# Sums of squares of a head from two rounded parts, four pieces of work at other places, and gates of 516 instead of 528 columns

## What is computed

```python
# a head of block one, and of block two alike
o = o * lax.rsqrt(jnp.mean(o * o, axis=-1, keepdims=True) + EPS)
o = o.reshape(...) * norm_w
out_a = (o * jax.nn.silu(g))
...
# Mamba-2: gate by z, mean square over each of two groups of 512 channels
y = y.reshape(bsz, length, M2_WIDTH) * jax.nn.silu(z)
yg = y.reshape(bsz, length, M2_GROUPS, M2_WIDTH // M2_GROUPS)
yg = yg * lax.rsqrt(jnp.mean(yg * yg, axis=-1, keepdims=True) + EPS)
...
h = h + jnp.concatenate([out_a, out_b], axis=-1) @ w_out
...
return y[:, N_META:, :]
```

## Time and profile before

| what | value |
|---|---|
| three runs, us | 1803.2, 1803.99, 1805.36 |
| the profiled execution: its time, us | 1804.95 |
| the profiled execution: its span, first to last instruction, us | 1803.2 |
| mean granted TensorE clock, share of full | 0.995 |
| PE busy, us (share of the span) | 1770.3 (98%) |
| DVE, ACT, POOL busy, us | 1168.4, 709.7, 10.4 |

### The profile page before, as it was taken

How to read it: one execution, slowest core, us unless ns; L and a number is a source line. 1 busy time by engine, 2 the same in 40 slices (tenths; PEclk the granted TensorE clock), 3 DMA queues, 4 the chain that set the end, 5 groups by cost and what they waited for, 6 DMA issues and landing times.

```text
span 1803.2 us, 27256 instructions
## 1 busy us (share of the span) xinstructions
PE 1770.3 (98%) x11004; PEld 1534.0 (85%) x11004; DVE 1168.4 (65%) x1798; ACT 709.7 (39%) x1085; POOL 10.4 (1%) x10
## 2 busy tenths in 40 slices
PE   8999999999999999999999999999999999999997
PEld 5777777778878888888899989999988999999885
DVE  5666656656567777633576766688788877777333
ACT  5333433332343333333545454543454433333221
POOL 0000000000000000000000000000000000000000
PEclk9999999999999999999999999999999999999998
DMA  6222222223333333332222122222212223333331
GB/s 200 79 74 79 82 82 84 82 81 94 93 87 98 96 94 93 103 96 94 70 84 71 59 69 63 70 71 63 79 60 80 74 94 94 95 94 87 101 93 59
DMA packets 44540, 154.23 MB, mean 86 GB/s; under 512 B 6000, under 2 KB 6256, under 8 KB 44416
## 3 DMA queue, kind: packets, MB, share of 16 engines
q1 hardware_dynamic: 44416, 152.50, 27.8%
HBM read 150.39 MB, written 2.10 MB: 85 GB/s over the span
## 4 chain that ended last, share of the span: by engine, by line
PE 81%; DVE 9%; ACT 4%; issue 2%; DVEq 1%; ACTq 1%; DMA 0%; POOL 0%; POOLq 0%; SPq 0%
PE ps L607 80%; ACT arena L911 2%; DVE arena L1272 2%; PE ps L611 2%; DVE w_lo L1269 1%; DVE arena L1279 1%; DVEq L1774 1%; ACTq L1252 1%; ACT w_hi L911 1%; DVE r_bc L1269 1%; ACT L916 0%; DVE arena L1269 0%; DVE u_lo L1464 0%; ACT u_hi L911 0%; DVE h_res L1269 0%
## 5 line engine op out<-in xcount | busy, mean ns | idle before, releaser
L607 PE MATMUL ps<-u_hi,w_hi 128*128 128x264 f32 (+3 forms) x2376 | 649.3, 326 | 12.1 <-DVE u_lo L1464 8.8
L607 PE MATMUL ps<-u_hi,w_lo 128*128 128x264 f32 (+3 forms) x2376 | 641.5, 323 | 0.0
L607 PE MATMUL ps<-u_lo,w_hi 128*128 128x264 f32 (+3 forms) x2376 | 639.9, 323 | 0.0
L607 PEld LDWEIGHTS ps<-u_hi,w_hi 128*128 128x128 f32 (+1 forms) x2376 | 395.9, 189 | 58.2 <-issue 14.7
L1269 DVE TENSOR_TENSOR w_lo<-w_raw,w_hi 128x1024 fp32r<-128x1024 f32 x280 | 342.5, 1223 | 153.6 <-ACT w_hi L911 142.2
L607 PEld LDWEIGHTS ps<-u_hi,w_lo 128*128 128x128 f32 (+1 forms) x2376 | 395.3, 188 | 36.9 <-issue 1.8
L607 PEld LDWEIGHTS ps<-u_lo,w_hi 128*128 128x128 f32 (+1 forms) x2376 | 395.1, 188 | 36.4 <-issue 0.8
L911 ACT ACTIVATE w_hi<-w_raw 128x1024 fp32r<-128x1024 f32 x280 | 294.7, 1053 | 327.4 <-PE ps L607 319.0
L1279 DVE SCALAR_TENSOR_TENSOR ffn<-full,par,ffn 128x512 f32<-128x512 f32 (+2 forms) x176 | 132.3, 751 | 81.0 <-ACT ffn L911 77.8
L911 ACT ACTIVATE arena<-arena 128x528 f32<-128x528 f32 (+10 forms) x189 | 96.5, 533 | 216.0 <-DVE arena L1272 91.8
L911 ACT ACTIVATE ffn<-full,par 128x512 f32<-128x512 f32 x88 | 67.8, 770 | 277.9 <-DVE full L1272 277.9
(11 more groups left out here) (140 smaller groups left out, 1488.2 us busy)
## 6 DMA issues: line engine op xcount, KB each, us to landing
w_raw<-weights SPq DMA_DIRECT2D x280, 512.0 KB, 3.6
h_res<-xT SPq DMA_DIRECT2D x8, 256.0 KB, 4.9
outT<-h_res SPq DMA_DIRECT2D x8, 256.0 KB, 2.1
cst<-consts SPq DMA_DIRECT2D x1, 730.0 KB, 8.6
seg<-consts SPq DMA_DIRECT2D x1, 256.0 KB, 8.7
par<-params SPq DMA_DIRECT2D x1, 240.0 KB, 5.7
msk<-cmask SPq DMA_DIRECT2D x1, 128.0 KB, 9.0
h_res<-metaT SPq DMA_DIRECT2D x1, 64.0 KB, 8.5
```

The lines of the kernel that those rows point to most:

```text
L607: return nc.tensor.matmul(out, lhsT, rhs, start=start, stop=stop)
```

## The change

**The head's sum.** Behind the copies of `head_c` ACT waits for its own squares and writes their rounded part into the head's place in `y_hi` (block one) or `v_hi` (block two), which is free at that time. A new DVE step `square_low` writes the rest into `y_lo` or `v_lo`. PE multiplies a column of rounded ones, repeated 128 times, with both parts. In block one `square_low` stands behind `head_c`; in block two inside the next head's `prep`, for the last head behind group ("mz", 0).

**Narrower.** Groups hg and mz and all that is done with gates, heads' roots and Mamba outputs cover columns 12 to 527.

**Four moves.** (1) the memsets `second_start 4` from behind hf 0 to behind hq 0; (2) ACT's `slab_behind` of group ("oh", 2) behind step a of tile 1; (3) ACT's tanh of group ("mz", 4) and its `slab_behind` behind `ssm_sum 0`; (4) on DVE the reading of group ("om", (0, 4)), and on ACT and POOL the square of tile 6, behind step a of tile 7. Besides, the scratch tile `m_cbm` lies elsewhere in the arena.

```diff
-    ... ("mz", 6): "silu mx 7; c 6", ("om", (0, 4)): "a 7",
+    ... ("mz", 6): "silu mx 7; c 6", ("om", (0, 4)): "a 7; sq 6; out 4",
@@ columns
-    return (USED, T2) if kind in ("oh", "om", "up2") else (0, T2)
+    return (USED, T2) if kind in ("oh", "om", "up2", "hg", "mz") else (0, T2)
@@ schedule
             put(*where, ("head_" + stage, h))
+            if stage == "c":
+                put(*where, ("square_low", h))
...
-    put("hf", 0, ("second_start", 4))
+    put("hq", 0, ("second_start", 4))
...
-                pieces += [("ssm_sum", 0)] if n == 4 else []
+                pieces += [("ssm_sum", 0), ("z_tanh", 4), ("slab_behind", GROUP_OF[where])] if n == 4 else []
                 pieces.append(("ssm_gate", n))
                 pieces += [("ssm_v2", n)] if n == M2_T - 1 else []
-                pieces.append(("ssm_sq", n))
+                pieces += [("ssm_sq", n)] if n != 6 else []
+            if where == ("oh", 2) and stage == "a":
+                pieces.append(("slab_behind", GROUP_OF[where]))
...
+    after[GROUP_OF[("mz", 0)]].append(("square_low", last))
@@ tensor engine, head_d
-                pe.wait_ge(o_ok, n + 1)
-                last = mm(ps[:, 6, :], ones[:, :], g_osq if gla else h_osq[:, META:T2])
+                pe.wait_ge(sq_lo_ok, n + 1)
+                _, hi, lo = square_parts(n)
+                m = 0 if gla else META - USED
+                every = ones_r[:, :].broadcast_to((P, P))
+                mm(ps[:, 6, :], every, hi[:, m:], stop=False)
+                last = mm(ps[:, 6, :], every, lo[:, m:], start=False)
                 if not gla:
-                    last = mm(ps[:, 7, 416:432], ones[:, :], h_osq[:, 0:META])
+                    mm(ps[:, 7, 416:420], every, hi[:, 0:m], stop=False)
+                    last = mm(ps[:, 7, 416:420], every, lo[:, 0:m], start=False)
@@ scalar engine
-                if GROUPS[g][0] != "hf":
+                if GROUPS[g][0] != "hf" and GROUPS[g][:2] not in (("mz", 4), ("oh", 2)):
                     slab_behind(g)
...
                 last.then_inc(o_ok, 1)
+                act.wait_ge(o_ok, n + 1)
+                x, hi, _ = square_parts(n)
+                f(hi, x, ACT.Copy).then_inc(sq_hi_ok, 1)
@@ vector engine, prep
                 last.then_inc(ready, 1)
+                if i:
+                    square_low(n - 1)
                 dve.wait_ge(act_part, PART_NO[GROUP_OF[("hg", i)]])
...
+            def square_low(n):
+                dve.wait_ge(sq_hi_ok, n + 1)
+                x, hi, lo = square_parts(n)
+                tt(lo, x, hi, ALU.subtract).then_inc(sq_lo_ok, 1)
```

More of the change, by code:

```diff
@@ L477, in program @@
         m_cb = take(2, NBLK, BLK, at_=o2 + 10 * P)
-        m_cbm = take(2, META, at_=o2 + 18 * P)
-        o2 += 18 * P + 2 * META
+        m_cbm = take(2, META, at_=10 * T2 + 2 * NBLK * M2_H + 2 * M2_H + 48)
+        o2 += 18 * P
         m_x = take(2, T2, at_=o2)
@@ L551, in residual_ready, with square_parts @@
                 evacuated(eng, GROUP_OF[({"g_ffn": "wo", "norm1": "down", "final": "down2"}[which], k)])
+        def square_parts(n):
+            if n < GLA_H:
+                return g_osq, y_hi[:, n, :], y_lo[:, n, :]
+            return h_osq[:, USED:], v_hi[:, n - GLA_H, USED:], v_lo[:, n - GLA_H, USED:]
         def main(v):
@@ L595, in ssm_sq @@
                     pool.wait_ge(ssm_sem["added"], 3 * (t // 4) + t % 4 - 1)
-                total = m_sq[:, t // 4, :]
-                nc.gpsimd.tensor_tensor(total, total, m_z[t % 2], ALU.add).then_inc(ssm_sem["added"], 1)
+                total = m_sq[:, t // 4, USED:]
+                nc.gpsimd.tensor_tensor(total, total, m_z[t % 2][:, USED:], ALU.add).then_inc(ssm_sem["added"], 1)
             for kind, i in STEPS:
@@ L886, in ssm_sum @@
                 mm(ps[:, 5, :], ones[:, :], m_sq[:, g, META:T2])
-                mm(ps[:, 6, 384:400], ones[:, :], m_sq[:, g, 0:META]).then_inc(S["sum"], 1)
+                mm(ps[:, 6, 384:388], ones[:, :], m_sq[:, g, USED:META]).then_inc(S["sum"], 1)
             def last_norm(which):
@@ L950, in group @@
                         act.wait_ge(gate2_ok, i)
-                    gate = (g_gate if kind == "gr" else h_gate)[:, i % 2, :]
+                    gate = g_gate[:, i % 2, :] if kind == "gr" else h_gate[:, i % 2, USED:]
                     evacuated(act, g)
-                    f(c_a if kind == "gr" else h_thg, gate, ACT.Tanh, scale=0.5).then_inc(act_part, 1)
+                    f(c_a if kind == "gr" else h_thg[:, USED:], gate, ACT.Tanh, scale=0.5).then_inc(act_part, 1)
                 elif kind == "hf":
@@ L992, in group, with z_tanh @@
                     f(sp[0:M2_R, :], sp[0:M2_R, :], ACT.Ln, bias=ones[0:M2_R, 0:1]).then_inc(ssm_sem["dt"], 1)
[L993 to L998, removed]
+                elif kind == "mz" and i != 4:
+                    z_tanh(i)
+            def z_tanh(i):
+                if i >= 2:
+                    act.wait_ge(ssm_sem["gated"], i - 1)
+                evacuated(act, GROUP_OF[("mz", i)])
+                f(full[:, i % 2, USED:], m_z[i % 2][:, USED:], ACT.Tanh, scale=0.5).then_inc(act_part, 1)
             def conv1(which):
@@ L1156, in head_d @@
                     f(h_or[:, META:T2], ps[:, 6, :], ACT.Ln, scale=1.0 / P, bias=pc("eps"))
-                    link(f(h_or[:, 0:META], ps[:, 7, 416:432], ACT.Ln, scale=1.0 / P, bias=pc("eps")))
-                    last = f(h_or, h_or, ACT.Exp, scale=-0.5)
+                    link(f(h_or[:, USED:META], ps[:, 7, 416:420], ACT.Ln, scale=1.0 / P, bias=pc("eps")))
+                    last = f(h_or[:, USED:], h_or[:, USED:], ACT.Exp, scale=-0.5)
                 last.then_inc(r_ok, 1)
@@ L1226, in ssm_sq @@
                 out = m_z[t % 2] if t % 4 else m_sq[:, t // 4, :]
-                f(out, m_y[:, t, :], ACT.Square).then_inc(S["sq"], 1)
+                f(out[:, USED:], m_y[:, t, USED:], ACT.Square).then_inc(S["sq"], 1)
                 if t == M2_T - 1:
@@ L1234, in ssm_v2 @@
                 act.wait_ge(S["gated"], t + 1)
-                f(v_hi[:, t, :], m_y[:, t, :], ACT.Identity, scale=pc("m2norm", t)).then_inc(S["v2hi"], 1)
+                f(v_hi[:, t, USED:], m_y[:, t, USED:], ACT.Identity, scale=pc("m2norm", t)).then_inc(S["v2hi"], 1)
             def ssm_sum(g):
@@ L1241, in ssm_sum @@
                 f(r[:, META:T2], ps[:, 5, :], ACT.Ln, scale=1.0 / SEQ, bias=pc("eps"))
-                link(f(r[:, 0:META], ps[:, 6, 384:400], ACT.Ln, scale=1.0 / SEQ, bias=pc("eps")))
-                f(r, r, ACT.Exp, scale=-0.5).then_inc(S["r"], 1)
-            stages = {"raw": raw, "raw_meta": raw_meta, "slab": lambda s: split_until(s + 1), "square": square, "norm": norm, "bounds": bounds, "group": group_and_slab, "prep": prep, "prep_ln": prep_ln, "prep_exp": prep_exp, "slab_behind": slab_behind, "gate_tanh": gate_tanh, "head_a": head_a, "head_b": head_b, "head_c": head_c,
+                link(f(r[:, USED:META], ps[:, 6, 384:388], ACT.Ln, scale=1.0 / SEQ, bias=pc("eps")))
+                f(r[:, USED:], r[:, USED:], ACT.Exp, scale=-0.5).then_inc(S["r"], 1)
+            stages = {"raw": raw, "raw_meta": raw_meta, "slab": lambda s: split_until(s + 1), "square": square, "norm": norm, "bounds": bounds, "group": group_and_slab, "prep": prep, "prep_ln": prep_ln, "prep_exp": prep_exp, "slab_behind": slab_behind, "z_tanh": z_tanh, "gate_tanh": gate_tanh, "head_a": head_a, "head_b": head_b, "head_c": head_c,
                       "head_d": head_d, "swa_v": swa_v, "swa_a": swa_a, "swa_b": swa_b, "ssm_dt": ssm_dt,
@@ L1299, in low_until @@
                 if until == 1:
-                    V.memset(ones[:, :], 1.0).then_inc(zeroed, 1)
+                    link(V.memset(ones[:, :], 1.0))
+                    V.tensor_copy(ones_r[:, :], ones[:, 0:1]).then_inc(zeroed, 1)
                 for s in range(low[0], until):
@@ L1359, in group @@
                     mul(vf1 if kind == "gv" else vf2, x, r).then_inc(free, 1)
-                elif kind in ("gr", "hg"):
-                    mul((g_gate if kind == "gr" else h_gate)[:, i % 2, :], x, r).then_inc(free, 1)
+                elif kind == "gr":
+                    mul(g_gate[:, i % 2, :], x, r).then_inc(free, 1)
+                elif kind == "hg":
+                    mul(h_gate[:, i % 2, USED:], x, r).then_inc(free, 1)
                 elif kind == "hf":
@@ L1406, in group @@
                     madd(tile, x, 0.5, tile).then_inc(free, 1)
[L1407 to L1413, removed]
+                elif kind == "om" and i != (0, 4):
+                    om_add(i)
                 elif kind in ("down", "oh", "down2"):
@@ L1435, in group, with om_add @@
                         dve.wait_ge(S["added"], 3 * ((i - 2) // 4) + (i - 2) % 4)
-                    mul(m_z[i % 2], x, r).then_inc(free, 1)
+                    mul(m_z[i % 2][:, USED:], x, r).then_inc(free, 1)
+            def om_add(i):
+                g2, m = i
+                g = GROUP_OF[("om", i)]
+                c0, c1 = columns(g)
```

(18 more changed lines are left out.)

15 lines of the change are left out of this document (9 added, 6 removed), and 2 rows, old and new, of the table SSM_PIECES.

## The result

The changed kernel takes 1793.94 us (median of 6 runs, 1792.36 to 1797.45) against 1803.93 for the kernel before (6 runs, 1803.2 to 1805.36): a ratio of 0.9945, interval 0.9935 to 0.9955. The six executions fall into two groups, three at 1792.36 to 1792.48 with a mean granted clock of 0.996 and three at 1795.4 to 1797.45 with 0.991 to 0.993; the median lies between them, and the profiled execution, 1796.02 with a span of 1794.2, is of the second.

What follows compares the result with a forecast made beforehand. PE, busy 98% of the span, was taken to bound the kernel. Terms 3.3 + 0.4 + 1.4 + 2.6 - 1.7 - 1.6 gave 4.4 us gained, so a median of 1799.6 us, range 1796.4 to 1802.8.

Steps and rivals of the forecast that it cites:

- The step that failed: Start of the kernel: rounding one column of ones costs nothing, since DVE waits for data there anyway.
- Sums and narrower groups: Head sums gain 3.3 in block two and 0.4 in block one; groups hg and mz gain 1.4.
- a full gain for the eighth head: Block two: each of eight heads, the last included, saves 0.41 on its sum, 3.3 together.
- In block one the wait: PE's wait for DVE at 113.23 grows from 0.34 to 0.75, so only the last head's 0.41 counts.
- The narrower groups: PE, 258 columns instead of 264: 0.125 per group, counted for hg 1 to 7 and mz 0 to 3, 1.4.
- Move 2: Tile 1: PE's wait falls from 1.47 to 0.6, gaining 0.87; the clock staying up gains 1.7; together 2.6.
- Move 1: Start of block two: PE's waits gather at 927.01, about 2.3; half clock behind it loses 1.7 (bounds 0 and 1.7).
- Moves 3 and 4: Behind tile 4 and at tile 7: PE idles 3.4, then up to 2; 1.6 lost in all (bounds 0.6 and 2.6).
- the rest of a POOL add: Tile 7: DVE's add, beside POOL's of tile 6, could stand this long by the skill page, up to 1 us more.
- The new wait: Rival: block two's low part comes late for PE, 3.6 slower when 1.0 is waited per head, 1807.6; chance 0.06.
- The first rival: Waits keep the clock up, nothing lost at 927, 0.6 instead of 1.6 behind tile 4: gain 7.1, 1796.9; chance 0.25.
- The moves bring nothing: Rival: the clock falls at tile 1 all the same, 2.6 lost behind tile 4: gain 1.7, 1802.3; chance 0.23.

Runs made afterwards that it cites:

- b_pad32: The kernel before with an unused 32-byte tile where the change puts its column of ones, `m_cbm` and arena length as changed; 1794.02 us, ratio 0.9946.
- a_m2wide: As a_m2, but groups hg and mz are 528 columns wide on PE again; 1789.76 us, ratio 0.9916 to the kernel before.
- a_m2: The changed kernel with only Move 2 of its four moves, the others undone; 1789.09 us, ratio 0.9913 to the kernel before.
- a_m0: The changed kernel without any of its four moves, keeping head sums and narrower work; 1790.11 us, ratio 0.9919 to the kernel before.
- b_ffnpad: The kernel before with 32 unused bytes only ahead of `a_hi` and `a_lo`; 1797.17 us, ratio 0.9963.
- b_u32p32: The kernel before with 32 unused bytes ahead of `u_hi` and 32 more behind `w_lo`; 1795.22 us, ratio 0.9944.
- a_m23: The changed kernel with only moves 2 and 3, the other two undone; 1791.87 us, ratio 0.9926 to the kernel before.
- b_w32p32: The kernel before with 32 unused bytes ahead of `w_raw` and 32 more behind `w_lo`; 1795.54 us, ratio 0.9947.

## Why the prediction was wrong

**The step that failed.** It is the sentence "The rounding of the ones is one column at the start, where DVE waits for data anyway: nothing." It priced the instructions and not the tile. Its 32 bytes moved all later tiles, and that is 9.9 us by the times of b_pad32 and 9.3 by the distances of starts, more than twice the rest of my sum. That the kernel became faster at all is luck: a_oldplace, the same edits at the old places, took 1804.28, which lies above the range as 1793.94 lies below it. So the sum of the edits was wrong as well. I had also taken 0.231 as what such a product costs, when it depends on where its operands lie; the earlier trace rows lie in `y`, in the worse place. The Trainium skill, TensorE: Matmul & The Clock Gate, section "Wait — 56ns, not 53.3ns?", gives 0.216 for 512 columns, and I noted the gap to 0.231 without asking what made it: the runs show 0.2267 as the lowest average of an operand's 512-column products, and still not 0.216.

**What was left of the sum.** Forecast -4.4, measured -0.1 (after beside b_pad32; a_oldplace beside before, at +0.4, says the same within its interval). By its terms:

- *Sums and narrower groups, 5.1 forecast; 3.9 to 4.9 measured.* The head's sum and the period are as forecast, 0.60 and 31.4. Part of what is missing is at the last head. There ACT's long dt step stands ahead of its root, and PE, now early, waits 0.66 for ACT. The kernel before has no such wait. I counted a full gain for the eighth head without looking at this chain: one head's gain and a half goes into it.

```profile
1134.66 0.43 PE L619 MATMUL ps<-arena 128*32 128x32 f32 x8 [0.66 <-ACT arena L928]
```

 In block one the wait grew by 0.15 and not 0.41. The instructions that make the rounded ones show no cost: PE's first product comes at 8.23 to 8.61 in the kernels with them and at 8.11 to 8.50 in those without. The narrower groups, 1.4 forecast, are 0.7 by the medians (a_m2wide beside a_m2): less than can be told from nothing.
- *Move 2, 2.6 forecast; 1.0 measured.* The wait went from 1.42 in a_m0 to 0.66: 0.76 of the 0.87 forecast. The 1.7 for the clock was the error. a_m0's trace has the wait of 1.42 and full clock behind it:

```profile
1208.64 1.35 PE L617 MATMUL ps<-arena 16*128 16x128 f32 x8 [1.42 <-DVE arena L1292]
```

```profile
1213.00:1218.00 5.00, 5.00 (x61) 4.66 (x59) 4.64 (x11) 0.52 (x1) 0.00 (x0) 1.00 0.30 102
```

 I had read one stretch of half clock (the 1.2 GHz level) as what the wait always does. Ten traces of the study have this wait, of 1.38 to 1.47. In three of them, before, b_ffnpad and b_u32p32, the clock falls behind it (the mean is 0.66 to 0.67 over 5 us); in the other seven it does not. Most of these are different kernels with the same wait, but one kernel varies too: on chip 5, executions of the kernel before with a mean clock of 0.998 took 1802.84 to 1803.15, those with 0.995 took 1805.01 and 1805.56.
- *Move 1, a loss of 1.7 forecast; 1.5 measured.* By the mechanism forecast: in the trace of after the wait gathers at the first `head_b`, with 0.66 as the clock's mean behind it. All three traces with move 1 have that fall of the clock, and none of the fifteen without.
- *Moves 3 and 4, a loss of 1.6 forecast, 2.6 as the bound; 3.4 to 4.7 measured.* The 1.6 was already high for its terms: 0.9 to 1.6, plus 0.2, less 0.3 is 0.8 to 1.5. Move 3 does what was said. ACT's second table load comes at 1304.99, tanh ends at 1306.92, and DVE waits 1.96 for it; its reading of om (0, 0) ends at 1311.04, and PE has waited 3.52. In a_m0 PE waits 1.49 for `r` and 0.24 at mx 6, so the stand is 1.8 longer.

```profile
1304.99 1.28 ACT L928 ACT_TABLE_LOAD   x1
1306.29 0.63 ACT L928 ACTIVATE full<-arena 128x516 f32<-128x516 f32 x1
...
1306.95 0.70 DVE L1308 SCALAR_TENSOR_TENSOR arena<-full,arena 128x516 f32<-128x516 f32 x1 [1.96 <-ACT full L928]
...
1310.34 0.70 DVE L1291 TENSOR_TENSOR h_res<-h_res,arena 128x516 f32<-128x516 f32 x1
```

 I let DVE regain 0.95 of this; by the distances above, 1.7 of the 1.8 was still there at the end. Of move 4 I said that the add takes 1.12 beside POOL "before and after". After, it is the four column products (two of 512 columns, two of 16) that lie beside POOL's add, and they take 2.53 where the same four took 1.45 at tile 1; the add has its 0.70. All that is lost is in the last product, of 16 columns: it starts 0.54 into POOL's add, takes 1.23 instead of 0.16, and ends 0.02 behind it. So a delay that I allowed for the add, "the rest of a POOL add", fell on a step that stands ahead of the reading that PE waits for. That is 1.08 lost for 0.42 regained, and 2.69 of PE's time at om (0, 5). Behind it the clock's mean is 0.66 over 10 us, 3.4 us lost, where my bound for the lower clock lay 1.0 above the forecast. How much of the loss is the clock's is not separated: a_m2 has as much of the lower clock between tile 4 and `a` as a_m23 has, and is 1.7 faster there.

```profile
1210.25 1.45 DVE L1294 TENSOR_TENSOR arena<-arena 128x512 f32<-128x512 f32 x4 [0.51 <-ACT arena L928]
...
1359.88 2.53 DVE L1294 TENSOR_TENSOR arena<-arena 128x512 f32<-128x512 f32 x4 [0.52 <-ACT arena L928]
...
1363.24 0.70 DVE L1291 TENSOR_TENSOR h_res<-h_res,arena 128x516 f32<-128x516 f32 x1
```

```profile
1360.64 1.75 POOL L609 TENSOR_TENSOR arena<-arena 128x516 f32<-128x516 f32 x1 [27.03 <-ACT arena L928]
```

**The rivals.** The new wait did not come. The first rival's 1796.9 is nearest in number but wrong in cause: the clock did fall at 922, and the stretch behind tile 4 cost more. Of the edits themselves "The moves bring nothing" comes nearest, but its 1.7 is still more than the 0.1 measured; the four moves together cost 3.8 by the medians, 4.7 by the ratios. The lower end of the range was also mis-added: the first rival less 0.1 for each of eight heads is 1796.1, not 1796.4.

**What stays open.** The products of `u` are at 0.2318 to 0.2321 on average in eleven of the twelve traces compared. Its blocks are 2112 bytes long, so their starts go through 0 and 64 modulo 128 in turn, and by the table about half should be quick. Within a group of eight units their distances do differ by place, from 0.226 to 0.236 in the trace of before, but not by every other unit. Only in b_w32p32 do `u` and the weights lie 32 or 96 apart, and there `u` is slower, 0.2327, as the relation says; the time shows no loss from it (1795.54 beside the 1795.22 of b_u32p32). Why `m` does not share the gain of `a` at 64, and which part of the chip makes the relation matter, the runs do not show either.

## What to carry to other kernels

When a change adds, drops or resizes a tile, work out where every later tile lands, and compare the distance of starts of untouched matmuls before and after. An unused tile of the same size in the kernel before is the experiment that tells placement from edit, and it belongs ahead of all others. Price a stretch of half clock as something that may come behind a wait, not as a part of it; and before moving a step on an engine that is full, look at what it will then share the time with.

## What was not expected of the hardware

- Fp32r products of 512 columns of `a` and `m` start every 0.2267 us when the moving operand and the weights start at the same place within 128 bytes, and every 0.2333 when 32 or 96 bytes lie between them: 2.8% of PE's time for them. With 64 between them it is 0.231 for `a` and 0.2333 for `m`.
- A wait of 1.38 to 1.47 us at tile 1 is followed by a window with a mean clock of 0.66 in three traces (the earlier trace rows is one) and by full clock in seven.
- A DVE product of 16 columns that began 0.54 us into a POOL add of 1.75 ended 0.02 behind it and took 1.23 instead of 0.16. A DVE product of 516 columns that read the accumulator took 0.69 beside such an add in before and 0.68 in a_m0, as it does without one.
